# A lower half in bf16 for 38 weight parts, and another order of the work around the attention and state-space outputs

## The chip, the cores and the metric

The program runs on one core of one Trainium2 chip. Its time is that of one execution on the device, in microseconds (us). Smaller is better. Five engines work beside each other, each through its own instructions in order, and wait for each other at semaphores: TensorE (PE in the profile, with its weight loads as PEld), VectorE (DVE), ScalarE (ACT), GpSimd (POOL) and SyncE (SP), which here only starts transfers.

## The reference

256 tokens of width 1024 go through two blocks. All is float32.

```
first block:   n1 = rmsnorm(x); proj = n1 @ w_in               # q k v r, low rank, su sv, ga gb
               h = x + (sig(ga)*(gla(q,k,v,r) @ wa) + sig(gb)*(sgu(su,sv) @ wb)) @ w_out
               n2 = rmsnorm(h)
               q  = n2 @ w_q                                   # peer: 8 heads, product keys
               idx, gates = top-16 of top-16 x top-16 scores, softmax
               h += sum_k gelu(n2 . U[idx_k]) * gates_k * V[idx_k]   # 16384 experts, run densely
second block:  h += norm(swiglu(norm(h)))                      # D_FF = 2816
               q,k,v,z,xbc,dt = norm(h) @ w_in_2
               attention: 8 heads, two softmaxes each, a = p1 - lam*p2; o = norm(a @ v) per head
               state space: conv, silu, chunks of 128 tokens, 16 heads; y = norm(y*silu(z)) per group
               h += norm([o, y] @ w_out_2)
               h += norm(swiglu(norm(h)))
```

## The kernel before, in words

**Products in three passes.** Weights arrive as float32 in items of 1 MB, each of two parts of 128 x 1024 (`load`, `stream`). ScalarE rounds each part to fp32r (`round_part`, L545: `whi`), another engine subtracts that from the original and keeps the rest (`rest_part`, L562: `wlo`). Activations are split in the same way by `stream_hi` (L1335) and `stream_lo` (L1836) into `XTh` and `XTl`. `products` (L713) then makes each product of three matmuls: high weight by high activation, high by low, low by high. There are three buffers for parts (`NBUF`), so ScalarE can round part p only when TensorE has finished part p-3; and raw items sit in a ring of three, released when both lower halves are made.

**Who makes the lower halves.** VectorE does, except for the 38 parts from `S_WQ + 2` to `S_EXP + POOLED - 1` (`pooled`): 14 parts of the query matrix `peer_wq` and the first 24 expert parts, which GpSimd makes while VectorE is at the top-16 searches (L1993 to L2005). Each of these parts is a `u_part`: 8 chunks of 128 rows by three matmuls, the weight loaded as the stationary operand, 256 tokens moving. After its searches VectorE waits for the last pooled part (`part_lo`) and goes on with the selection (L2039) and with its own parts.

**Order.** Each engine's program is written out by hand. `split_to(p)` makes an engine catch up with its half of the splits up to part p at that point of its program; `take(name)` and `after(name)` first do `split_to` two parts beyond the part that the named product follows (`USE_PART`), and then wait for the product, or for its being read. Products live in PSUM banks; `MAIN` lists them in order, `MAIN_BANK` deals banks 0 to 3 out in turn, and `claim` makes TensorE wait until the one before in that bank has been read. Transposes have banks of their own (`T_BANK`, `t_claim`).

**The stage of attention and state space.** Parts of this stage are named by panel: AK (keys, four parts, `by_feature`), AV (values, four), ZZ (gate z, eight, `by_token`), WM (output matrix, twelve). TensorE runs: AK parts; decays (L1141); the scores at0 to at15 with one AV part after each four; ZZ+0 to ZZ+3 (zz0, zz1); the products inside a chunk yd0, yd1 (L1176); the state st0, st1 (L1185); three groups of transposed probabilities (L699, stage `pt`); yo0, yo1 (L1194); three more; ZZ+4; the attention products ao0, ao1 (L1203); ZZ+5 to ZZ+7; the transposed attention output; yd2, yd3; WM+0 to WM+3; the transposed state-space output (stage `ssm`); WM+4 to WM+11. `pt` uses four banks, and ScalarE copies all six groups out (L1657). `ssm` uses four banks too. VectorE makes the probabilities ready in four rounds (`normalise`, L2455 to L2467), between these its parts and bank reads (`within_tokens`, L2475, yo at L2489), then scales the attention output (L2505). ScalarE has the exponentials (L1639), the gate's silu (`z_gate`, L1649), and the squares for both norms (L1672, L1666).

Of the kernel before, what the change touches and what calls it, by code (L numbers as in the profile page):

```python
# [7 lines left out]
P = 128  # L8
# [169 lines left out]
_use(("yd0", "dve"), ("yd1", "dve"), ("st0", "act"), ("st1", "act"), ("yo0", "dve"), ("yo1", "dve"))  # L178
_part()
_use(("ao0", "dve"), ("ao1", "dve"))  # L180
_part(), _part(), _part(main="zz3"), _use(("zz2", "act"), ("zz3", "act"))
_use(("yd2", "dve"), ("yd3", "dve"))
# [10 lines left out]
SAME_BANK = {"ao0": "yo0", "ao1": "yo1"}  # L193
MAIN_BANK, _n = [], 0
for _name, _ in MAIN:
    if _name in SAME_BANK:
        MAIN_BANK.append(MAIN_BANK[MAIN_AT[SAME_BANK[_name]]])
    else:
        MAIN_BANK.append(OWN_BANK.get(_name, _n % 4))
        _n += _name not in OWN_BANK  # L200
# [19 lines left out]
def before_in(ring, n):  # L220
# [6 lines left out]
          "ffa": S_FFA - 2, "mix": S_MIX - 2, "dtt": S_MIX + 1, "xs": S_AK - 1, "bm": S_AK - 1, "pt": S_ZZ + 4, "att": S_WM - 1,  # L227
# [8 lines left out]
FOUR_BANKS = {"n1", "ya", "yb", "mg", "n2", "ffa", "mix", "pt", "ffb"}  # L236
SSM_BANKS = (6, 7, MAIN_BANK[MAIN_AT["yd2"]], MAIN_BANK[MAIN_AT["yd3"]])
T_BANK = []
for _name, _k in TSTAGES:
    for _j in range(_k):  # L240
        _i = T_AT[_name] + _j
        if _name in FOUR_BANKS:
            T_BANK.append((6, 7, 4, 5)[(_j + 2 * (_name == "yb")) % 4])
        else:
            T_BANK.append(SSM_BANKS[_j] if _name == "ssm" else 6 + _i % 2)

# [9 lines left out]


def reader_of(stage, j):

    return 1 if stage == "pt" else (T_AT[stage] + j) % 2  # L260
# [7 lines left out]
def program(nc, x, panels1, experts, ffa, panels2, ffb, cols, conv_cols, w_low, w_gate_up, w_sgu, k12, w_dt,  # L268
# [9 lines left out]
    with ctx:  # L278
# [77 lines left out]
        cut = Cut(TAIL_AT + NK * T // 2 + NBUF * PART // 2)  # L356
# [70 lines left out]
        xt_hi, xt_lo = sem("xt_hi"), sem("xt_lo")  # L427
# [65 lines left out]
        def t_read_wait(eng, i):  # L493

            for stage, pairs in TSTAGES:
                j = i - T_AT[stage]
                if 0 <= j < pairs:
                    if stage in STREAMS:
                        eng.wait_ge(xt_lo, STREAM_AT[stage] + j + 1)
                    else:  # L500
                        before = sum(1 for s2, n2 in TSTAGES if s2 not in STREAMS for k in range(n2)
                                     if T_AT[s2] + k <= i and reader_of(s2, k) == reader_of(stage, j))
                        eng.wait_ge(t_read[reader_of(stage, j)], before)
# [7 lines left out]
        def t_mine(who, stage, pairs):  # L511

            return [j for j in range(pairs) if reader_of(stage, j) == who]
# [171 lines left out]
        def _(pe):  # L685
            def transposes(stage, srcs, norm=None, waits=None, pieces=None, scales=None, pairs=None):

                for j in pairs or range((len(srcs) + 3) // 4):
# [231 lines left out]
            for h in range(PEER_H + 1):  # L920
                if h < PEER_H:
# [265 lines left out]
            read_out(pe, "av1")  # L1187
            probabilities = [PR[:, h // 2, 2 * (h % 2), P * j:P * j + P] for h in range(AT_H) for j in range(3)]
            normalised = lambda j: (att_a, (4 * j + 3) // 6 + 1)
            transposes("pt", probabilities, waits=normalised, pairs=range(3))  # L1190
# [5 lines left out]
            transposes("pt", probabilities, waits=normalised, pairs=range(3, 6))  # L1196
            token_part(["zz2", "zz3"], S_ZZ + 4, 0)
            t_read_all(pe, "pt", 6)
            for tt in range(NT):
# [23 lines left out]
        def _(act):  # L1223
# [409 lines left out]
            for r in range(4):  # L1633
                split_to(S_AV + r + 2 + max(r - 1, 0))
# [24 lines left out]
            warm_root(3)  # L1659
# [40 lines left out]
        def _(dve):  # L1700
# [286 lines left out]
            stream_lo("n2")  # L1987

# [446 lines left out]
            for r in range(4):  # L2435
# [7 lines left out]
                if r == 3:  # L2443
                    split_to(S_AV + 5)
# [4 lines left out]
                split_to(S_AV + r + 2 + 2 * (r == 3))  # L2449
# [21 lines left out]
            def within_tokens(i):  # L2471

                b = arrived(dve, f"yd{i}")
# [4 lines left out]
            normalise(1)  # L2478
            link(dve.tensor_tensor(SMALL[:, 0, :], DT[:, 0, :], ECUM[:, 2, :], ALU.mult))
            dve.tensor_tensor(by_head(XDS), by_head(XS[:, 0, :]), over_head(SMALL[:, 0, :]), ALU.mult).then_inc(xds_ready, 1)  # L2480
            normalise(2)
            within_tokens(0)
            within_tokens(1)
            normalise(3)
            split_to(S_ZZ + 4)
            for g in range(2):
                b = arrived(dve, f"yo{g}")
# [3 lines left out]
            split_to(S_ZZ + 5)  # L2491
            weights(1)
            split_to(S_ZZ + 6)

            for tt in range(NT):
                if tt:
                    split_to(S_ZZ + 7)
# [14 lines left out]
            after("zz3")  # L2512
            dve.tensor_tensor(XS[:, 0, :], XS[:, 0, :], Z[:, 0, :], ALU.mult).then_inc(ssm_gated, 1)
            split_to(S_WM + 2)
# [3 lines left out]
            link(dve.tensor_tensor(XS[:, 1, :], XS[:, 1, :], YOFF, ALU.add))  # L2518
# [99 lines left out]
```

## Time and profile before

| | |
|---|---|
| time, median of 3 runs | 1593.77 us (1591.63 to 1594.12) |
| the profiled execution's own time | 1591.63 us |
| its span, first to last instruction | 1589.9 us |
| mean granted clock of TensorE | 0.998 |
| PE busy | 1555.1 us, 98% of the span, 9128 matmuls |
| DVE busy | 1254.3 us, 79% |
| ACT busy | 806.0 us, 51% |
| POOL busy | 105.1 us, 7% |
| transfers | 270.43 MB, mean 170 GB/s |

The profile is one execution. Matmuls overlap in the pipeline, so the rate of TensorE is read from the distance of starts, not from the length of one matmul.

### The profile page before, as it was taken

To read this page: it belongs to the slowest core of one execution; us is meant where nothing else is said; L and a number is where in the kernel's file an instruction comes from. 1 tells how busy PE (TensorE), PEld (TensorE's weight loads), DVE (VectorE), ACT (ScalarE), POOL (GpSimd) and SP (SyncE) were. 2 spreads that over 40 slices of the span, in tenths; PEclk is the share of its full clock that TensorE was granted. 3 is DMA by queue.
4 is the path that set the end of the run, shared out by engine and by line. 5 is a ranking of instruction groups with operands and counts; after the bars stand their busy time and mean duration, and the time that the engine had idled before them with its cause. 6 is when DMAs were issued, how large, how long until landed. Compare 5 with 4: busy or idle time off the path is not lost.

```text
span 1589.9 us, 26306 instructions
## 1 busy us (share of the span) xinstructions
PE 1555.1 (98%) x9128; PEld 1364.0 (86%) x9128; DVE 1254.3 (79%) x2169; ACT 806.0 (51%) x1231; POOL 105.1 (7%) x67
## 2 busy tenths in 40 slices
PE   8999899999999999999999999999999999999998
PEld 7888799999999888888888888888887988778886
DVE  5575669989999777777777777888888988688877
ACT  5545545457776343344444444544445667554443
POOL 0000177700000000000000000000000000000000
PEclk9999999999999999999999999999999999999999
DMA  5545444532334555545555555555554433445552
GB/s 225 192 154 173 156 144 169 182 142 108 106 109 181 194 202 185 189 181 188 192 195 190 185 185 185 197 204 185 185 185 154 165 119 110 155 173 185 185 189 101
DMA packets 39387, 270.43 MB, mean 170 GB/s; under 512 B 4882, under 2 KB 5394, under 8 KB 7075
## 3 DMA queue, kind: packets, MB, share of 16 engines
q1 hardware_dynamic: 37440, 266.45, 47.1%
q10 hardware_dynamic: 1890, 3.24, 0.6%
q8 instruction: 34, 0.56, 0.1%
q14 instruction: 23, 0.18, 0.0%
HBM read 268.62 MB, written 1.05 MB: 170 GB/s over the span
## 4 chain that ended last, share of the span: by engine, by line
PE 79%; DVE 15%; issue 3%; ACT 2%; DVEq 1%; DMA 0%; SPq 0%; ACTq 0%
PE ps L713 51%; PE ps L746 16%; PE ps L748 7%; DVE wlo L562 2%; DVE raw L2079 2%; DVE wlo L2108 2%; PE ps L745 1%; DVE whi L2079 1%; DVE wlo L2079 1%; DVE XT L1836 1%; ACT whi L545 1%; DVE raw L2092 1%; DVE arena L2441 0%; PE ps L699 0%; PE ps L1141 0%
## 5 line engine op out<-in xcount | busy, mean ns | idle before, releaser
L746 PE MATMUL ps<-XT,whi 128*128 128x512 f32 x1200 | 429.2, 398 | 2.3 <-DVE XT L1836 1.7
L713 PE MATMUL ps<-XT,whi 128*128 128x256 f32 x1696 | 310.9, 285 | 1.1 <-DVE wlo L562 1.1
L748 PE MATMUL ps<-XT,wlo 128*128 128x256 f32 x1050 | 294.5, 280 | 0.0
L713 PE MATMUL ps<-whi,HAh 128*128 128x512 f32 x696 | 272.3, 391 | 2.4 <-DVE HAl L2267 1.4
L713 PE MATMUL ps<-wlo,HAh 128*128 128x512 f32 x696 | 271.2, 390 | 0.0
L713 PE MATMUL ps<-whi,HAl 128*128 128x512 f32 x696 | 270.8, 389 | 0.0
L545 ACT ACTIVATE whi<-raw 128x1024 fp32r<-128x1024 f32 x182 | 191.4, 1058 | 155.2 <-PE ps L713 125.8
L713 PEld LDWEIGHTS ps<-XT,whi 128*128 128x128 f32 x1696 | 263.7, 192 | 1.7 <-DVE wlo L562 1.5
L746 PEld LDWEIGHTS ps<-XT,whi 128*128 128x128 f32 x1200 | 222.5, 188 | 48.4 <-issue 2.1
L562 DVE TENSOR_TENSOR wlo<-raw,whi 128x1024 fp32r<-128x1024 f32 x162 | 196.6, 1222 | 72.4 <-ACT whi L545 70.7
L713 PE MATMUL ps<-XT,wlo 128*128 128x256 f32 x848 | 239.8, 283 | 0.0
L1559 ACT ACTIVATE whi<-raw 128x1024 fp32r<-128x1024 f32 x108 | 114.7, 1062 | 175.2 <-PE ps L746 114.3
L748 PEld LDWEIGHTS ps<-XT,wlo 128*128 128x128 f32 x1050 | 198.2, 189 | 5.7
L713 PE MATMUL ps<-whi,XT 128*128 128x512 f32 x592 | 184.7, 393 | 3.3 <-DVE XT L1836 1.4
L2306 DVE TENSOR_TENSOR wlo<-raw,whi 128x1024 fp32r<-128x1024 f32 x108 | 132.0, 1222 | 49.6 <-ACT whi L1559 48.3
L713 PEld LDWEIGHTS ps<-XT,wlo 128*128 128x128 f32 x848 | 162.4, 191 | 0.0
L713 PEld LDWEIGHTS ps<-wlo,HAh 128*128 128x128 f32 x696 | 130.6, 188 | 28.1
L713 PEld LDWEIGHTS ps<-whi,HAl 128*128 128x128 f32 x696 | 130.7, 188 | 27.9
L713 PEld LDWEIGHTS ps<-whi,HAh 128*128 128x128 f32 x696 | 130.9, 188 | 27.4 <-issue 3.3
L713 PEld LDWEIGHTS ps<-whi,XT 128*128 128x128 f32 x592 | 109.5, 188 | 30.3 <-issue 4.7
L2176 DVE TENSOR_TENSOR wlo<-raw,whi 128x1024 fp32r<-128x1024 f32 x108 | 130.8, 1221 | 1.1
L713 PE MATMUL ps<-wlo,XT 128*128 128x512 f32 x296 | 115.4, 390 | 0.0
(293 smaller groups left out, 1919.5 us busy)
## 6 DMA issues: line engine op xcount, KB each, us to landing
raw<-in_experts SPq DMA_DIRECT2D x128, 1024.0 KB, 4.8
raw<-in_panels SPq DMA_DIRECT2D x58, 1024.0 KB, 4.8
raw<-in_ffa SPq DMA_DIRECT2D x33, 1024.0 KB, 4.7
raw<-in_ffb SPq DMA_DIRECT2D x33, 1024.0 KB, 4.8
arena<-in_row_post ACTq DMA_DIRECT2D x3, 512.0 KB, 4.7
X<-in_x SPq DMA_DIRECT2D x2, 512.0 KB, 5.2
arena<-in_row_ln ACTq DMA_DIRECT2D x2, 256.0 KB, 4.2
arena<-in_row_post SPq DMA_DIRECT2D x1, 512.0 KB, 5.6
```

The lines of the kernel that those rows point to most:

```text
L545: act.activation(whi[:, buf(p), :], half(item_of(p), p % 2), ACT.Copy).then_inc(part_hi, 1)
L562: eng.tensor_tensor(low_weights(p), half(item_of(p), p % 2), whi[:, buf(p), :].bitcast(f32), ALU.subtract).then_inc(part_lo, 1)
L713: last = pe.matmul(out, x if w_moving else w, w if w_moving else x, start=start and n == 0, stop=stop and n == 2)
L745: pe.matmul(out[:, T:], wl[:, k], XTh[:, k], start=False, stop=False)
L746: last = pe.matmul(out, wh[:, k], XT[:, k], start=k == 0, stop=k == NK - 1)
L748: pe.matmul(out[:, T:], wl[:, k], XTh[:, k], start=False, stop=False)
L1559: act.activation(whi[:, buf(q), :], half(item_of(q), q % 2), ACT.Copy)\
L1836: last = dve.scalar_tensor_tensor(lo, t_bank(stage, j)[:, T * q:T * q + T], col(gain, k) if gain else 1.0, hi.bitcast(f32), ALU.mult, ALU. ...
L2079: return dve.tensor_tensor(out, iota.bitcast(f32).unsqueeze(1).broadcast_to(shape), idx[:, bass.ds(g * ONES, n)].unsqueeze(2).broadcast_to ...
L2108: dve.tensor_tensor(wlo[:, buf(p), :], half(item_of(p), p % 2), whi[:, buf(p), :].bitcast(f32), ALU.subtract).then_inc(part_lo, 1)
L2176: dve.tensor_tensor(wlo[:, buf(p + j), :], half(item_of(p), j), whi[:, buf(p + j), :].bitcast(f32), ALU.subtract).then_inc(part_lo, 1)
L2306: dve.tensor_tensor(wlo[:, buf(q), :], half(item_of(q), q % 2), whi[:, buf(q), :].bitcast(f32), ALU.subtract).then_inc(part_lo, 1)
```

## The change

It has two parts. First, the 38 pooled parts get a lower half in bf16 (`WB1`) in place of fp32r, VectorE makes a bf16 copy of the high activations (`XB1`, 128 x 2048) once, and the third pass multiplies these two. TensorE waits for that copy at the second query panel. Second, the order of the attention and state-space stage differs: which part is split where, which product comes when, which bank it has, and who copies the transposed probabilities out. The diff is condensed: calls stand side by side, and some bodies are named instead of printed.

```diff
 # banks and bookkeeping
-_use(("yd0","dve"), ("yd1","dve"), ("st0","act"), ("st1","act"), ("yo0","dve"), ("yo1","dve"))
-_part()
-_use(("ao0","dve"), ("ao1","dve"))
-_part(), _part(), _part(main="zz3"), _use(("zz2","act"), ("zz3","act"))
-_use(("yd2","dve"), ("yd3","dve"))
+_use(("yd0","dve"), ("yd1","dve"), ("st0","act"), ("st1","act"))
+_by_token("zz2", "zz3", "act")
+_use(("yo0","dve"), ("yo1","dve"), ("ao0","dve"), ("ao1","dve"), ("yd2","dve"), ("yd3","dve"))
-SAME_BANK = {"ao0": "yo0", "ao1": "yo1"}
-# pt: four banks, read by ScalarE alone; ssm: banks 6, 7 and those of yd2, yd3
+# pt and ssm: banks 6 and 7 in turn; pt read by VectorE and ScalarE in turn
 # bf16
+        XB1 = cut(NK * T // 2).bitcast(bf16).rearrange("p (k t) -> p k t", k=NK)
+        WB1 = cut(NBUF * PART // 2).bitcast(bf16).rearrange("p (b n) -> p b n", b=NBUF)
 def low_weights(p):
+            if pooled(p):
+                return WB1[:, buf(p), :]
             return wlo[:, buf(p), :]
 def third_acts(p):
+            if pooled(p):
+                return XB1
             return XTh
 # TensorE
+                if h == 1:
+                    pe.wait_ge(xt_b, 1)
 ...
-            read_out(pe, "av1");  transposes("pt", probabilities, pairs=range(3))
+            by_token(["zz2", "zz3"], S_ZZ + 4)
             read_out(pe, "st1");  yo0, yo1
-            transposes("pt", probabilities, pairs=range(3, 6))
-            token_part(["zz2", "zz3"], S_ZZ + 4, 0)
+            transposes("pt", all six)
             t_read_all(pe, "pt", 6);  ao0, ao1
-            for j in range(1, 4):
-                token_part(["zz2", "zz3"], S_ZZ + 4, j)
+            within_tokens(1)
             pe.wait_ge(att_y, 1)
             transposes("att", tiles(AOUT, 4))
-            within_tokens(1)
 # ScalarE
-                split_to(S_AV + r + 2 + max(r - 1, 0))
+                split_to(S_AV + r + 2 + (r == 3))
 ...            z_gate(0); st0, st1
+            z_gate(1)
+            warm_root(3)
             pt copies (now every second one)
-            warm_root(3)
             for tt in range(NT):  ao square
-                split_to(S_ZZ + 7)
             head_root(2, 16)
-            act.activation(warm[4], ident[:, 0:1], ACT.Silu)
-            z_gate(1)
+            ssm_squares(0)
             stream_hi("att")
-            warm_root(0)
-            ssm_squares(0)
 # VectorE
             stream_lo("n2")
+            dve.tensor_copy(XB1, XTh.bitcast(f32)).then_inc(xt_b, 1)
 ...            XSKIP, c = 0, 1
-                if c == 0:
-                    split_to(S_AK + 2)
 ...            scores
-                if r == 3:
-                    split_to(S_AV + 5)
-                split_to(S_AV + r + 2 + 2 * (r == 3))
+                split_to(S_AV + r + 2)
             normalise(0)
-            normalise(1);  xds
-            normalise(2);  within_tokens(0), (1)
-            normalise(3);  split_to(S_ZZ + 4);  yo reads;  split_to(S_ZZ + 5)
-            weights(1);  split_to(S_ZZ + 6)
+            split_to(S_ZZ + 2);  xds;  split_to(S_ZZ + 3)
+            normalise(1);  split_to(S_ZZ + 4)
+            normalise(2);  split_to(S_ZZ + 5);  within_tokens(0), (1)
+            normalise(3);  split_to(S_ZZ + 6)
+            weights(1);  split_to(S_ZZ + 7)
+            after("zz3");  XS0 * Z0;  yo reads
+            pt copies 0, 2, 4
             attention sums, head_scale, AOUT, stream_lo("att")
-            after("zz3");  XS0 * Z0;  split_to(S_WM + 2)
             within_tokens(2), (3);  + YOFF
-            XS1 * Z1;  split_to(S_WM + 3)
+            split_to(S_WM + 3);  XS1 * Z1
```

## Rows read from the trace of the kernel before

**Rows 1.** Windows: length; busy PE, PEld, DVE, ACT, POOL; granted clock; transfer share; GB/s.

```profile
237.00:337.00 100.00, 100.00 (x837) 100.00 (x836) 94.95 (x331) 48.02 (x70) 63.26 (x26) 1.00 0.51 179
1292.00:1372.00 80.00, 78.36 (x471) 63.67 (x470) 66.16 (x120) 56.39 (x131) 0.00 (x0) 1.00 0.29 107
```

**Rows 2.** Timeline of PE, query panels and experts: start, us, operation [idle before].

```profile
222.89 0.28 PE L713 MATMUL ps<-XT,wlo 128*128 128x256 f32 x1
...
228.28 0.28 PE L713 MATMUL ps<-XT,wlo 128*128 128x256 f32 x1
...
599.38 0.39 PE L713 MATMUL ps<-wlo,HAh 128*128 128x512 f32 x1
...
605.50 0.39 PE L713 MATMUL ps<-wlo,HAh 128*128 128x512 f32 x1
```

**Rows 3.** Timelines of DVE and POOL, first block.

```profile
210.19 0.88 DVE L1993 MAX8 arena<-arena 128x8 f32<-128x128 f32 x4 [11.23 <-ACT arena L1412]
...
257.55 2.40 POOL L562 TENSOR_TENSOR wlo<-raw,whi 128x1024 fp32r<-128x1024 f32 x1 [0.26 <-ACT whi L545]
...
314.87 1.43 DVE L2039 SCALAR_TENSOR_TENSOR arena<-arena 128x256 bf16<-128x256 f32 x4 [2.63 <-POOL wlo L562]
...
348.82 0.42 DVE L2058 COPY sel<-ps 128x256 f32<-128x256 f32 x1 [1.33 <-PE ps L699]
```

**Rows 4.** Timelines of PE and DVE at the AK parts.

```profile
1280.20 0.48 PE L713 MATMUL ps<-XT,whi 128*128 128x256 f32 x2
...
1284.69 1.22 DVE L562 TENSOR_TENSOR wlo<-raw,whi 128x1024 fp32r<-128x1024 f32 x1
1285.82 1.22 DVE L2427 TENSOR_TENSOR arena<-arena 128x1024 f32<-128x1024 f32 x1
```

**Rows 5.** Timeline of DVE from the last scores to the attention output.

```profile
1315.73 2.36 DVE L562 TENSOR_TENSOR wlo<-raw,whi 128x1024 fp32r<-128x1024 f32 x2
1317.99 0.20 DVE L2455 RECIPROCAL arena<-arena 128x8 f32<-128x8 f32 x1
...
1320.86 0.20 DVE L2455 RECIPROCAL arena<-arena 128x8 f32<-128x8 f32 x1
...
1327.94 1.28 DVE L2475 TENSOR_TENSOR arena<-arena,ps 128x512 f32<-128x512 f32 x2
...
1344.02 1.29 DVE L2505 TENSOR_TENSOR arena<-ps,arena 128x512 f32<-128x512 f32 x2
```

**Rows 6.** Timeline of ACT, third round of exponentials and the splits after it.

```profile
1310.59 0.39 ACT L1639 ACTIVATE arena<-arena 128x128 f32<-128x128 f32 x1
...
1314.10 2.16 ACT L545 ACTIVATE whi<-raw 128x1024 fp32r<-128x1024 f32 x2
```

**Rows 7.** Timeline of PE through the stage.

```profile
1323.10 3.68 PE L1176 MATMUL ps<-arena 128*128 128x64 f32 x32
...
1328.38 1.47 PE L699 MATMUL ps<-ident,arena 128*128 128x128 f32 x12
1329.69 1.88 PE L1194 MATMUL ps<-arena 128*128 128x512 f32 x4
...
1336.22 5.46 PE L1203 MATMUL ps<-arena 128*128 128x64 f32 x48
...
1349.79 1.03 PE L699 MATMUL ps<-ident,arena 128*128 128x128 f32 x8
...
1354.15 0.71 PE L713 MATMUL ps<-whi,XT 128*128 128x512 f32 x2
...
1365.66 1.91 PE L699 MATMUL ps<-ident,arena 128*128 128x128 f32 x16
1368.26 0.70 PE L713 MATMUL ps<-whi,XT 128*128 128x512 f32 x2 [0.70 <-DVE XT L1836]
```

**Rows 8.** Windows after two gaps of PE, the columns of rows 1.

```profile
1220.00:1222.00 2.00, 2.00 (x11) 1.88 (x10) 2.00 (x6) 1.71 (x5) 0.00 (x0) 0.50 0.00 0
...
1394.00:1396.00 2.00, 1.36 (x11) 0.92 (x10) 1.68 (x4) 1.57 (x4) 0.00 (x0) 1.00 0.00 0
```

More of the change, by code:

```diff
@@ L177 @@
 _by_token("zz0", "zz1", "act")
-_use(("yd0", "dve"), ("yd1", "dve"), ("st0", "act"), ("st1", "act"), ("yo0", "dve"), ("yo1", "dve"))
-_part()
-_use(("ao0", "dve"), ("ao1", "dve"))
-_part(), _part(), _part(main="zz3"), _use(("zz2", "act"), ("zz3", "act"))
-_use(("yd2", "dve"), ("yd3", "dve"))
+_use(("yd0", "dve"), ("yd1", "dve"), ("st0", "act"), ("st1", "act"))
+_by_token("zz2", "zz3", "act")
+_use(("yo0", "dve"), ("yo1", "dve"), ("ao0", "dve"), ("ao1", "dve"), ("yd2", "dve"), ("yd3", "dve"))
 assert _parts == S_WM
@@ L192 @@
 OWN_BANK = {"av0": 4, "av1": 5, "wm0": 4, "wm1": 5}
-SAME_BANK = {"ao0": "yo0", "ao1": "yo1"}
 MAIN_BANK, _n = [], 0
 for _name, _ in MAIN:
[L196 to L200, printed above, removed]
+    MAIN_BANK.append(OWN_BANK.get(_name, _n % 4))
+    _n += _name not in OWN_BANK
 I_G, I_PRE = EXP0 + FIRST // 2, EXP0 + EARLY // 2
@@ L234 @@
     _n += _k
-FOUR_BANKS = {"n1", "ya", "yb", "mg", "n2", "ffa", "mix", "pt", "ffb"}
-SSM_BANKS = (6, 7, MAIN_BANK[MAIN_AT["yd2"]], MAIN_BANK[MAIN_AT["yd3"]])
+FOUR_BANKS = {"n1", "ya", "yb", "mg", "n2", "ffa", "mix", "ffb"}
 T_BANK = []
@@ L241 @@
         _i = T_AT[_name] + _j
[L242 to L245, printed above, removed]
+        T_BANK.append((6, 7, 4, 5)[(_j + 2 * (_name == "yb")) % 4] if _name in FOUR_BANKS else 6 + _i % 2)
 STREAMS = {"n1": (0, "norm1"), "ya": (0, "gla"), "yb": (4, None), "mg": (0, None), "n2": (0, "norm2"),
@@ L511, in t_mine @@
         def t_mine(who, stage, pairs):
-            return [j for j in range(pairs) if reader_of(stage, j) == who]
+            return [j for j in range(pairs) if (T_AT[stage] + j) % 2 == who]
         def item_of(p):
@@ L685, in _, with transposes @@
         def _(pe):
-            def transposes(stage, srcs, norm=None, waits=None, pieces=None, scales=None, pairs=None):
-                for j in pairs or range((len(srcs) + 3) // 4):
+            def transposes(stage, srcs, norm=None, waits=None, pieces=None, scales=None):
+                for j in range((len(srcs) + 3) // 4):
                     t_claim(pe, stage, j)
@@ L1186, in _ @@
                           stop=True).then_inc(main_done, 1)
[L1187 to L1190, printed above, removed]
+            by_token(["zz2", "zz3"], S_ZZ + 4)
             read_out(pe, "st1")
@@ L1195, in _ @@
                           stop=True).then_inc(main_done, 1)
-            transposes("pt", probabilities, waits=normalised, pairs=range(3, 6))
-            token_part(["zz2", "zz3"], S_ZZ + 4, 0)
+            transposes("pt", [PR[:, h // 2, 2 * (h % 2), P * j:P * j + P] for h in range(AT_H) for j in range(3)],
+                       waits=lambda j: (att_a, (4 * j + 3) // 6 + 1))
             t_read_all(pe, "pt", 6)
+            read_out(pe, "av1")
             for tt in range(NT):
@@ L2471, in within_tokens @@
             def within_tokens(i):
[L2473 removed]
+                b = take(f"yd{i}")
                 c, half_c = i // 2, slice(512 * (i % 2), 512 * (i % 2) + 512)
@@ L2484, in _ @@
             normalise(3)
-            split_to(S_ZZ + 4)
+            split_to(S_ZZ + 6)
+            weights(1)
+            split_to(S_ZZ + 7)
+            after("zz3")
+            dve.tensor_tensor(XS[:, 0, :], XS[:, 0, :], Z[:, 0, :], ALU.mult).then_inc(ssm_gated, 1)
             for g in range(2):
-                b = arrived(dve, f"yo{g}")
+                b = take(f"yo{g}")
                 e = ECUM[:, 1, 8 * g:8 * g + 8].unsqueeze(2).broadcast_to([P, 8, SSM_P])
```

31 lines of the change are left out of this document (14 added, 17 removed).

## The prediction, made before the changed kernel ran

> **What bounds the kernel now.** I read the page's busy times first, then windows, then the timelines of single engines. TensorE is the bound almost everywhere, and in both places that the change touches: between 237 and 337 us, in the pooled parts, it is busy for all of the 100 us, and between 1292 and 1372 us for 78.36 of 80 [rows 1]. So two things count: what shortens TensorE's own work, and what makes it wait. The second window also says how little a better order could give there: 1.6 us of idle time.
>
> **Part one, the bf16 pass.** A part in the pooled stretch is 24 matmuls of 256 columns. Third-pass matmuls start at 222.89 and 15 triplets later at 228.28, 5.39 / 45 = 0.120 us each. With 512 columns, 27 matmuls take 605.50 - 599.38 = 6.12 us, 0.227 each [rows 2]. The difference is 0.107 us per 256 columns, so each matmul costs its columns plus a fixed 0.0133 us. The columns stay, and bf16 can take away at most the fixed piece. The changed matmuls are 38 parts x 8 chunks = 304, so the gain lies between 0 and 304 x 0.0133 = 4.0 us. No row shows a bf16 matmul, or says how much of the fixed piece belongs to the four-byte operands. It stands at both widths, so it is not streaming, and the operand's size is what changes: I take three quarters, 0.010 us and **-3.0 us** in all, and keep 0 and 4.0.
>
> The Trainium skill has a price for this (TensorE: Matmul & The Clock Gate, section on the 56 ns): a warm bf16 matmul starts N / 2.4 GHz + about 2.5 ns after the one before. By it the step is 0.109 us and the gain 304 x 0.0108 = 3.3 us. The same page (Weight-path perf modes) has bf16 weights of 128 columns loaded faster than float32 ones, which cannot take the step below its columns; no run here shows either yet.
>
> Is the gain kept? GpSimd needs 2.40 us a part and the shortest gap before one is 0.26 [rows 3], 2.66 us, against a new TensorE period of 24 x 0.120 - 8 x 0.010 = 2.80 us. It keeps up if writing bf16 costs it no more than 0.14 us. VectorE waits 2.63 us for the last pooled part at 314.87, so it can follow up to that much, and at 348.82 it sits waiting for TensorE's transposes after its selection, so it is not what is late there [rows 3]. The new copy of 128 x 2048 is bounded by twice a 128 x 1024 subtraction, 2 x 1.22 = 2.4 us; it lies in VectorE's 11.23 us of idle time before 210.19 [rows 3], which begins at 198.96 with the last streamed activation. TensorE takes these chunks up as they come, so at least one of the first panel's two parts (2.88 us) lies behind that moment and covers the copy. Cost nothing; without that cover, 2.4 us once, in front of the searches and in front of TensorE. TensorE's wait for it has nothing late behind it.
>
> **Part two, the order.** Here I walk the new programs through with the durations of the rows, in the time of the trace before. Units: a VectorE split 1.13 us (1315.73 to 1317.99 for two), one round of `normalise` 2.87 (1317.99 to 1320.86), reading two banks 1.2, one bank 0.6 [rows 5]; a round of exponentials 3.5 (1310.59 to 1314.10), a rounding by ScalarE 1.08 [rows 6]; a `by_token` part 12 x 0.227 = 2.72, yd plus st 5.28 (1323.10 to 1328.38), yo 1.7, ao 5.3, att transposes and yd 4.36 (1349.79 to 1354.15) of which yd is 3.5, the ssm stage 2.6 until WM+4 starts [rows 7].
>
> *AK+2.* TensorE starts this part at 1280.20 + 2 x 2.88 = 1285.96, and its lower half is made 1284.69 to 1285.91, just in time [rows 4]. The change puts the XSKIP product, 1.13 us, in front. TensorE starts at 1287.1: **+1.1**. The scores follow TensorE, so all behind it moves along.
>
> I leave this 1.1 out of the times that follow.
>
> *ZZ+0 to ZZ+3.* They start at 1323.10 - 4 x 2.72 = 1312.2 and every 2.72 us. ZZ+1 is wanted at 1314.9. ScalarE now rounds it behind the third exponentials, and these can start only one rounding sooner: I take them 1310.0 to 1313.5, ZZ+1 rounded at 1314.6. VectorE splits it until 1315.8: TensorE waits 0.9 and ends it at 1318.6. `normalise(0)` comes in between, and ZZ+2 is split at 1318.6 to 1319.8: wait 1.3. xds takes until 1321.1; ScalarE has the fourth exponentials, the AV copies, then ZZ+3 rounded at about 1321.3; VectorE splits by 1322.5; TensorE wants it at 1322.6. ZZ+3 ends at 1325.3 instead of 1323.10: **+2.2**.
>
> *zz2's bank.* yd and st run to 1330.6. zz2 and zz3 now lie in the banks of yd0 and yd1. VectorE, from 1322.4 with two rounds (5.74), two splits (2.26) and the reads (1.2), frees them at 1331.6: wait **+1.1**. Then ZZ+4 to ZZ+7 run 1331.7 to 1342.6, split in time.
>
> *The transposed probabilities.* VectorE must wait for zz3's silu (1343.5, a pipeline's end and 0.6 behind the last part), multiply (1.13), read yo (1.2) and only then copy pair 0, by 1346.5. TensorE has finished yo and two pairs at 1345.2 and the next pair needs that bank: wait 1.3. With two banks each further pair needs the copy before it, then the last must be copied before the attention products: 0.5 and 0.9 more. Sum **+2.7**; ao starts at 1349.65. Before, four banks and ScalarE alone hid it behind yo.
>
> *Attention output.* ao ends at 1354.95, yd2 and yd3 at 1358.45. The scaled output came 3.8 us after ao (1341.5 to 1345.3 [rows 5, 7]), so 1358.75: wait 0.3. Before, yd2 and yd3 lay between the att transposes and WM+0 and hid the streaming; now TensorE waits for it. The ssm stage shows that distance, 2.6 us from first transpose to next part: WM+0 starts at 1361.35 instead of 1354.15. The lateness was 6.0 (2.2 + 1.1 + 2.7); it is now 7.2: **+1.2**.
>
> *ssm with two banks.* WM+0 to WM+3, 4 x 2.72, end at 1372.2; the y scales are ready just before. Pair 2 then waits for the low half of pair 0, pair 3 for that of pair 1, 3.7 us in place of 2.6, and WM+4 starts at 1375.9 instead of 1368.26, 7.6 late: **+0.4**, since the stretch before WM+4 already held 0.6 us of waits (1354.15 to 1365.66 is 11.5 for 10.9 of work) that the late start swallows. WM+5 is split behind the stream, **+0.2**.
>
> Sum of the order: 1.1 + 2.2 + 1.1 + 2.7 + 1.2 + 0.4 + 0.2 = **+8.9 us**. A walk may be off by a wait or two of about 1.3 each: 6.5 to 11.
>
> **Total.** -3.0 + 8.9 = +5.9. The profiled execution took 1591.63 us for a span of 1589.9, so 1597.5 on its own time. The median of the runs is 2.1 above it: 1593.77 + 5.9 = **1599.7 us**, 0.37% slower.
>
> **The rivals.**
> (a) *The clock falls.* After the feed-forward before this stage, TensorE had a gap with only transposes in it, and the granted clock was 0.50 at 1220 to 1222, the 1.2 GHz level; after a similar gap at 1392 it stayed at 1.00 [rows 8]. In my walk the pt, att and ssm stretches each have 2 to 3 us of waits with nothing but transposes between. Half clock over some 4 us costs 2 us: 1601.7. For it: the same shape of gap; against: the even record. The Trainium skill (TensorE: Matmul & The Clock Gate, Part 4) says that a transpose does not count as TensorE being busy; by that rule the fall is likelier than the record says, and the time would be this one.
> (b) *bf16 changes nothing on TensorE.* The fixed piece stays at 0.0133: 1593.8 + 8.9 = 1602.7. For it: weights and moving columns are still 128 and 256, and two passes of three keep fp32r. Against: nothing else can explain why the piece is the same at both widths.
> (c) *GpSimd becomes the pace.* It decides from 2.54 us a part on. At a fifth more, 2.88 + 0.26 = 3.14 us against 2.88 now, 36 parts cost +9 instead of -3: 1612. Against: it writes half the bytes.
> (d) *The other side: not slower.* VectorE, idle for long stretches after 1338, is not late: it reaches yd0 before TensorE ends st (before 1330.6; my walk has 1331.6) and pair 0 before TensorE ends pair 1 (before 1345.2; my walk has 1346.5). Then the waits for zz2's bank and for pair 0, and those that follow from it, fall away, 1.1 + 2.7. The order costs 5.1, the whole +2.1: 1595.9, which a measurement cannot tell from no change; with the bf16 gain at its bound of 4.0 it is +1.2, and it is faster only if the stream waits go too. VectorE's chain is fixed in order, and at either place a whole us would have to be found, so this is unlikely.
>
> **How the numbers follow.** A difference of 0.2%, 3.2 us, is about what a measurement of this kernel can tell from no change. Forecast 0.50; (a) 0.20; (b) 0.10; (c) 0.05; (d) 0.12, all of it within 0.2%; faster, by (d) with everything going well, 0.03. Of the forecast a twentieth is left for an order that costs 6 or less. So slower 0.83, same 0.14, faster 0.03. The range takes in (a), (b) and most of (d), and the order's bounds: 1595.5 to 1605.
>
> **What would show it.** In the changed profile the third pass has bf16 operands and steps of 0.110 instead of 0.120 beside 0.120 for the others, a pooled part takes 2.80 us, and VectorE's wait before L2039 is near nothing. PE waits for DVE's splits at AK+2, ZZ+1 and ZZ+2 (0.9 to 1.3 each), for the reads of yd, for copies of L699's pairs, and before WM+0 for XT. The window from AK to WM+4 is 9 us longer. The prediction is wrong if the 0.0133 stays or GpSimd's part exceeds 2.54 us, or if VectorE and ScalarE are ahead of TensorE at the banks of yd0 and pair 0.

## The result, and the profile after

The changed kernel takes 1605.99 us in the median of five runs (1603.14 to 1611.96), the kernel before 1592.99 us (1591.63 to 1594.12) in its five beside it. The ratio is 1.0068, with a 95% interval of 1.0054 to 1.0084: slower, by 10.8 us. It is smaller than the 13.0 us between the two medians because it takes in all 31 executions of the changed kernel (1601.08 to 1611.96, median 1603.59), and not only these five. The forecast was +5.9 us. On the 1593.77 us that it was made against, the ratio gives 1604.6, inside the range of 1595.5 to 1605 by 0.4 us; the median of the five stands 1 us above it. The profiled execution took 1603.59 us for a span of 1601.8, with a mean granted clock of 0.994 where before had 0.998.

First the bf16 pass. PE's timeline of the changed kernel in the query panels, which answers to [rows 2]:

```profile
221.41 0.28 PE L703 MATMUL ps<-arena 128*128 128x256 bf16 x1
221.45 0.48 PE L703 MATMUL ps<-XT,whi 128*128 128x256 f32 x2
221.77 0.28 PE L703 MATMUL ps<-arena 128*128 128x256 bf16 x1
...
222.85 0.28 PE L703 MATMUL ps<-arena 128*128 128x256 bf16 x1
```

Four triplets lie between 221.41 and 222.85, so one takes 0.36 us and a matmul still 0.120 on average. Nothing has become shorter. The weight load of that pass has, in the groups of weight loads (line, operation, shapes, count | busy us, mean ns | idle before):

```profile
L703 PEld LDWEIGHTS ps<-XT,whi 128*128 128x128 f32 x1696 | 263.8, 193 | 2.9 <-DVE wlo L552 1.5 <-issue 1.3
...
L703 PEld LDWEIGHTS ps<-arena 128*128 128x128 bf16 x304 | 28.9, 95 | 12.8
```

It takes 95 ns instead of 193, but loads lie beside the matmuls, and the step does not follow them. The windows of the changed kernel (columns of [rows 1]) have TensorE busy for all of the pooled stretch, as before:

```profile
237.00:337.00 100.00, 100.00 (x838) 90.53 (x837) 94.88 (x342) 48.73 (x71) 64.22 (x27) 1.00 0.50 175
...
190.00:200.00 10.00, 7.47 (x46) 6.92 (x45) 5.74 (x15) 5.79 (x15) 0.00 (x0) 0.83 0.30 106
```

The second of these rows is code that both kernels share, and its granted clock is 0.83: it fell to 0.50 there for 3.4 us, and once more near 167 us. The profile of the kernel before has neither fall. The timelines of DVE and POOL, which answer to [rows 3]:

```profile
201.13 1.22 DVE L1973 CAST arena<-XT 128x2048 bf16<-128x2048 f32 x1
212.47 0.87 DVE L1979 MAX8 arena<-arena 128x8 f32<-128x128 f32 x4 [10.11 <-ACT arena L1400]
...
259.89 2.40 POOL L552 TENSOR_TENSOR arena<-raw,whi 128x1024 bf16<-128x1024 f32 x1 [0.30 <-ACT whi L531]
...
317.21 1.43 DVE L2025 SCALAR_TENSOR_TENSOR arena<-arena 128x256 bf16<-128x256 f32 x4 [2.64 <-POOL arena L552]
```

The copy of the activations took 1.22 us and is hidden: 10.11 us of idle time are left behind it. GpSimd writes bf16 in the same 2.40 us. VectorE waits 2.64 us for the last pooled part, as it did before (2.63), since no part has become shorter.

Then the order. PE's timeline from the AK panel to WM+5, which answers to [rows 4, 7]; brackets hold the idle time before an instruction and its releaser:

```profile
1282.57 0.48 PE L703 MATMUL ps<-XT,whi 128*128 128x256 f32 x2
...
1289.68 0.47 PE L703 MATMUL ps<-XT,whi 128*128 128x256 f32 x2 [1.13 <-DVE wlo L552]
...
1319.61 0.73 PE L703 MATMUL ps<-whi,XT 128*128 128x512 f32 x2 [0.88 <-DVE wlo L552]
1323.62 0.72 PE L703 MATMUL ps<-whi,XT 128*128 128x512 f32 x2 [0.99 <-DVE wlo L552]
1329.21 3.68 PE L1168 MATMUL ps<-arena 128*128 128x64 f32 x32
...
1335.34 0.70 PE L703 MATMUL ps<-whi,XT 128*128 128x512 f32 x2 [0.68 <-DVE arena L2457]
1346.34 1.88 PE L1183 MATMUL ps<-arena 128*128 128x512 f32 x4
...
1350.34 1.09 PE L689 MATMUL ps<-ident,arena 128*128 128x128 f32 x8 [1.25 <-DVE arena L2483]
1351.78 1.09 PE L689 MATMUL ps<-ident,arena 128*128 128x128 f32 x8 [0.35 <-DVE arena L2483]
1353.56 5.57 PE L1193 MATMUL ps<-arena 128*128 128x64 f32 x48 [0.69 <-ACT arena L1647]
...
1362.87 1.09 PE L689 MATMUL ps<-ident,arena 128*128 128x128 f32 x8 [0.17 <-DVEq L2499]
1365.48 0.70 PE L703 MATMUL ps<-whi,XT 128*128 128x512 f32 x2 [1.52 <-issue]
1379.00 1.44 PE L689 MATMUL ps<-ident,arena 128*128 128x128 f32 x8 [1.47 <-DVE XT L1821]
1383.57 0.74 PE L703 MATMUL ps<-whi,XT 128*128 128x512 f32 x2 [0.36 <-DVE wlo L552]
```

The reader should see two things. Every wait of the prediction is there, at the place it named. And the AK panel itself starts 2.37 us later than before (1282.57 against 1280.20), ahead of all changed order. So the measure for the order is the distance from the start of the AK panel to the start of WM+5: 101.00 us here, and 91.45 before, where WM+5 started so:

```profile
1371.65 0.74 PE L713 MATMUL ps<-whi,XT 128*128 128x512 f32 x2 [0.39 <-DVE wlo L562]
```

The order costs 9.55 us in this execution; the sum had 8.9. Below, that distance is called **AK to WM+5**. Behind WM+5 nothing differs: 1601.8 - 1383.57 = 218.2 us are left to the end of the span, and 1589.9 - 1371.65 = 218.3 before. So the spans of the two profiled executions differ by 11.9 us: 9.55 by the order, and 2.4 ahead of the AK panel, where the two falls lie. splits_back below, which has neither of these falls, starts its panel at 1280.70.

### The profile page after: what moved, and what is told of

The parts are those of the page before. It is cut to its first block, busy times and chain, and to the rows that moved or that the text cites. A ratio compares the mean times of both kernels' runs of the same rounds, so it can differ in the third digit from the quotient of the medians.

```text
span 1601.8 us, 26306 instructions
## 1 busy us (share of the span) xinstructions
PE 1560.6 (97%) x9128; PEld 1354.8 (85%) x9128; DVE 1257.6 (79%) x2173; ACT 802.7 (50%) x1224; POOL 105.4 (7%) x67
## 4 chain that ended last, share of the span: by engine, by line
PE 80%; DVE 14%; issue 3%; ACT 2%; DVEq 1%; DMA 0%; ACTq 0%
PE ps L703 52%; PE ps L736 16%; PE ps L738 7%; DVE wlo L552 2%; DVE wlo L2094 2%; DVE raw L2065 2%; PE ps L735 1%; DVE wlo L2065 1%; DVE whi L2065 1%; PE ps L689 1%; DVE XT L1821 1%; ACT whi L531 0%; DVE arena L2425 0%; PE ps L955 0%; PE ps L1133 0%
## 5 line engine op out<-in xcount | busy, mean ns | idle before, releaser
L738 PE MATMUL ps<-XT,wlo 128*128 128x256 f32 x1050 | 294.5, 280 | 0.0
L531 ACT ACTIVATE whi<-raw 128x1024 fp32r<-128x1024 f32 x182 | 191.4, 1057 | 163.0 <-PE ps L703 133.8
L738 PEld LDWEIGHTS ps<-XT,wlo 128*128 128x128 f32 x1050 | 198.3, 189 | 5.7
L1547 ACT ACTIVATE whi<-raw 128x1024 fp32r<-128x1024 f32 x108 | 114.7, 1062 | 175.2 <-PE ps L736 114.3
L703 PE MATMUL ps<-XT,wlo 128*128 128x256 f32 x544 | 153.8, 283 | 0.0
L1479 ACT ACTIVATE whi<-raw 128x1024 fp32r<-128x1024 f32 x60 | 63.8, 1063 | 99.4 <-PE ps L703 99.4
```

Source lines behind the costliest of these rows:

```text
L531: act.activation(whi[:, buf(p), :], half(item_of(p), p % 2), ACT.Copy).then_inc(part_hi, 1)
L703: last = pe.matmul(out, x if w_moving else w, w if w_moving else x, start=start and n == 0, stop=stop and n == 2)
L738: pe.matmul(out[:, T:], wl[:, k], XTh[:, k], start=False, stop=False)
L1479: act.activation(whi[:, buf(p), :], half(item_of(p), p % 2), ACT.Copy).then_inc(part_hi, 1)
L1547: act.activation(whi[:, buf(q), :], half(item_of(q), q % 2), ACT.Copy)\
```

## Experiments

**The bf16 pass alone, and the order alone.** The first is the kernel before with the hunks of `XB1` and `WB1` and nothing else, the second is the changed kernel without them:

```diff
 bf16_only: the kernel before
+            if pooled(p): return WB1[:, buf(p), :]      # low_weights
+            if pooled(p): return XB1                    # third_acts
+            dve.tensor_copy(XB1, XTh.bitcast(f32)).then_inc(xt_b, 1)
 order_only: the changed kernel
-            the same lines
```

> The kernel before with the bf16 third pass of the pooled parts alone. My theory after the result: three bf16 matmuls among fp32r ones keep the step of 0.120 us (a triplet stays at 0.36 us, a pooled part at 2.88), so the time is that of before, within 0.1% (1592 to 1594 us where before has 1593). The rival, the forecast of the prediction: the gain is real but hidden in the changed kernel by something else, a triplet takes 0.350 us, a part 2.80 and the time is 3.0 us shorter, ratio 0.998.

> The changed kernel with its third pass put back to fp32r, so the new order alone. My theory: all of the loss is the order, WM+5 starts 9.5 us later after the start of the AK panel than it did before, and the time is that of the whole change, ratio 1.006 (1601 to 1604 us, where a fall of the granted clock outside the changed code adds or takes about 2 us). The rival, that the bf16 pass gives 3.0 us which the order of the changed kernel loses too: ratio 1.008 to 1.009.

The bf16 pass alone: 1593.22 us against 1593.87, ratio 0.9999 (0.999 to 1.0008); AK to WM+5 is 91.41. It neither gives nor costs, as expected. The order alone: 1604.69 us, ratio 1.0073 (1.0061 to 1.0086), that of the whole change. Its profile has an AK to WM+5 of 102.53 us, and there the windows of PE (length, busy, granted clock, transfers) show why it is 1.5 more than in the changed kernel:

```profile
1364.00:1366.00 2.00, 1.34 (x11) 1.00 0.00 0
...
1368.00:1370.00 2.00, 2.00 (x6) 0.50 0.00 0
```

The granted clock fell to 0.50, the 1.2 GHz level, at WM+0, behind the attention products and the transposes. So the clock does fall in this stage in this execution, as in the prediction's rival (a).

**Where the fixed piece of a matmul sits.** The bf16 matmuls kept the 0.120 us step of the fp32r ones. Two kernels ask what holds it there. The first is the changed kernel, new order included, with every pass of the pooled parts in bf16; it leaves out the products with the high halves of those parts, so its output is another one. The second keeps the computation, and puts the eight bf16 matmuls of a part behind its sixteen fp32r ones.

```diff
 bf16_probe: the changed kernel, u_part
+                if pooled(p): wh = wl
+                acts = (x3[:, k],) * 3 if pooled(p) else (XTh[:, k], XTl[:, k], x3[:, k])
 bf16_grouped: the kernel before with the bf16 pass, u_part
+                if pooled(p):
+                    for k in range(NK):
+                        chunk_in(k)
+                        pe.matmul(out, wh[:, k], XTh[:, k], start=k == 0, stop=False)
+                        pe.matmul(out, wh[:, k], XTl[:, k], start=False, stop=False)
+                    for k in range(NK):
+                        last = pe.matmul(out, wl[:, k], x3[:, k], start=False, stop=k == NK - 1)
+                    return last
```

> The changed kernel in which all three passes of the pooled parts take bf16 weights and bf16 activations, so that every matmul of these parts is bf16; it leaves out the products with the high-rounded weights and the activations' streamed halves, whose places bf16 products of the same size take. If the fixed piece of 0.0133 us belongs to the operands' size and a neighbour in fp32r keeps it alive, the step falls to 0.107 to 0.110 and a part from 2.88 to 2.57 to 2.64 us. If the fixed piece belongs to every matmul whatever its type, the step stays 0.120 and the part 2.88. Where GpSimd needs 2.40 + 0.26 us a part, a faster TensorE shows as its waits for GpSimd's or VectorE's, of at most 0.1 us a part.

> The kernel before with the bf16 third pass, and in each pooled part the eight bf16 matmuls in a row behind the sixteen fp32r ones. The runs so far have a bf16 matmul at 0.120 us between fp32r ones and at 0.109 where all are bf16. Theory: what counts is the matmul next to it, so seven of the eight take 0.109, a part 2.80 us instead of 2.88, and 38 parts save 2.9 us: ratio 0.998, 1590 to 1591 us where before has 1593 to 1594. Rival one: fp32r work anywhere in the part keeps 0.120, or the change of type costs it again at the two borders, no gain, ratio 1.000. Rival two: GpSimd, at 2.66 us a part, or VectorE cannot follow, and TensorE's idle time grows by what the step gives.

PE's timeline of the first kernel:

```profile
254.81 4.42 PE L703 MATMUL ps<-arena 128*128 128x256 bf16 x39
```

39 matmuls take 4.42 us, of which the last has 0.28: (4.42 - 0.28) / 38 = 0.109 us each. The fixed piece falls from 0.0133 to about 0.002 when the neighbours are bf16 as well. The time was 1591.92 us in its one execution, 11.7 us below the changed kernel's profiled one; 38 parts of 24 such matmuls, 0.011 us less each, make 10 of these. The Trainium skill (TensorE: Matmul & The Clock Gate, section on the 56 ns) gives N / 2.4 GHz plus about 2.5 ns, an estimate of 0.109 us for 256 columns: the trace agrees, for bf16 beside bf16.

And PE's timeline of the second:

```profile
253.80 1.05 PE L743 MATMUL ps<-arena 128*128 128x256 bf16 x8
254.60 0.36 PE L740 MATMUL ps<-XT,whi 128*128 128x256 f32 x1
254.80 0.28 PE L741 MATMUL ps<-XT,whi 128*128 128x256 f32 x1
...
256.59 1.05 PE L743 MATMUL ps<-arena 128*128 128x256 bf16 x8
257.39 0.36 PE L740 MATMUL ps<-XT,whi 128*128 128x256 f32 x1
```

One part, from 254.60 to 257.39, takes 2.79 us instead of 2.88. That is 16 x 0.120 + 8 x 0.109, so the two changes of type in a part cost nothing. This kernel takes 1590.38 us against 1592.17, ratio 0.9983 (0.9974 to 0.9992), about 2.7 us, where 38 parts at 0.09 each make 3.4: the theory, that the matmul next to it counts, was right, and this kernel is faster than both. What it is in an fp32r neighbour that holds the step up, no run shows. AK to WM+5 is 91.37, so the gain lies ahead of the stage. The last wait of VectorE for a pooled part fell from 2.63 to 2.42 only, and GpSimd kept up.

**One wait made alone.** The kernel before, with the second XSKIP product ahead of the split of AK+2:

```diff
 ak_only: the kernel before
                 ins = dve.tensor_tensor(by_head(XSKIP[:, c, :]), ...)
-                if c == 0:
-                    split_to(S_AK + 2)
```

> The kernel before with one product by XSKIP moved in front of the split of AK+2. Both theories of the walk have TensorE wait for that split once: about 1.1 us (the changed kernel showed 1.13) at AK+2, and all that follows 1.1 us later up to WM+5. The rival: before WM+5 there is slack that takes it back, and WM+5 stands as far from the start of AK as in the kernel before.

```profile
1283.26 0.49 PE L713 MATMUL ps<-XT,whi 128*128 128x256 f32 x2
...
1290.38 0.48 PE L713 MATMUL ps<-XT,whi 128*128 128x256 f32 x2 [1.12 <-DVE wlo L562]
...
1375.94 0.72 PE L713 MATMUL ps<-whi,XT 128*128 128x512 f32 x2 [0.38 <-DVE wlo L562]
```

AK to WM+5 is 1375.94 - 1283.26 = 92.68, 1.23 more than before. Nothing behind it takes the wait back: the theory was right, its rival not. The panel starts late here too (1283.26), with clock falls in the same shared code; distances are free of that.

**Three moves undone one at a time, from the changed kernel.**

```diff
 splits_back: roundings and splits of ZZ and AV in the places they had before
-                split_to(S_AV + r + 2 + (r == 3))              # ScalarE
+                split_to(S_AV + r + 2 + max(r - 1, 0))
-                split_to(S_AV + r + 2)                         # VectorE
+                split_to(S_AV + r + 2 + 2 * (r == 3))          # and S_AV + 5 ahead of the last read
 pt_four: four banks for the transposed probabilities, ScalarE copies all six groups
 ssm_four: four banks for the ssm transposes
```

> The changed kernel with ScalarE's roundings and VectorE's splits of the ZZ and AV parts in the places that they had before. Theory: the waits of 0.88 and 0.99 us at ZZ+1 and ZZ+2 vanish, and VectorE then stands later at the bank of zz2 (0.68 us before): WM+5 is 1.5 to 2 us earlier. Rival: VectorE's chain is what is late behind it, the waits move on to the bank of zz2 and to pair 0, and less than 0.5 us comes back.

> The changed kernel with four banks for the transposed probabilities, all copied by ScalarE, as before. Theory: the waits of 1.25, 0.35 and 0.69 us of the changed trace come from VectorE, which reaches pair 0 late; without them the attention products start about 2.3 us earlier, but what follows (the scaled output, the streaming, the y scales) is late by itself and takes some of it back: WM+5 stands 1.3 us earlier behind the start of the AK panel than in the changed kernel (99.7 instead of 101.0 us). Rival one: all 2.3 come back. Rival two: ScalarE with four copies is as late as VectorE was, and nothing comes back.

> The changed kernel with four banks for the ssm transposes. Theory: the wait of 1.47 us before WM+4 goes and with it 1.1 us of the time up to WM+5. Rival: the y scales or the streaming of the lower halves are what is late there, and the wait moves to the next chunk with less than 0.3 us gained.

| kernel | AK starts | WM+5 starts | AK to WM+5 | against the change |
|---|---|---|---|---|
| before | 1280.20 | 1371.65 | 91.45 | -9.55 |
| the change | 1282.57 | 1383.57 | 101.00 | |
| splits_back | 1280.70 | 1381.51 | 100.81 | -0.19 |
| pt_four | 1283.57 | 1382.76 | 99.19 | -1.81 |
| ssm_four | 1283.28 | 1383.15 | 99.87 | -1.13 |

ssm_four gave what was expected (1.1). pt_four gave 1.81, between the 1.3 of its theory and the 2.3 of its first rival. splits_back gave almost nothing, against a theory of 1.5 to 2. PE's timeline of splits_back at zz2:

```profile
1333.32 0.69 PE L703 MATMUL ps<-whi,XT 128*128 128x512 f32 x2 [3.00 <-DVE arena L2459]
```

The waits of 0.88 and 0.99 at ZZ+1 and ZZ+2 are gone, and the wait for the bank of zz2 has grown from 0.68 to 3.00. Its releaser is the read of yd0 by VectorE. DVE's timeline of the changed kernel has that read here:

```profile
1333.95 1.28 DVE L2457 TENSOR_TENSOR arena<-arena,ps 128x512 f32<-128x512 f32 x2
```

It starts 51.38 us behind AK. In splits_back it starts at 1331.95, 51.25 behind AK. So VectorE's chain up to that read keeps its length, and TensorE waits for its end in one place or in three. In the kernel before the read started 1327.94 - 1280.20 = 47.74 us behind AK [rows 4, 5]. The 3.5 to 3.6 us between are the wait at AK+2 (1.2) and two splits of 1.13: by the diffs, VectorE has made the lower halves up to ZZ+3 ahead of this read in the kernel before, and up to ZZ+5 in the changed one and in splits_back. PE's timeline of pt_four, and that of ssm_four:

```profile
1352.78 5.57 PE L1198 MATMUL ps<-arena 128*128 128x64 f32 x48 [0.95 <-ACT arena L1652]
```

```profile
1379.76 0.70 PE L707 MATMUL ps<-whi,XT 128*128 128x512 f32 x2 [0.70 <-DVE XT L1825]
```

In pt_four the three waits of 1.25, 0.35 and 0.69 have become one of 0.95. In ssm_four the wait before WM+4 is 0.70, exactly that of the kernel before [rows 7].

**Is it the bank?** This is splits_back with zz2 and zz3 in the banks of av0 and av1:

```diff
 zz_own: splits_back, and
-OWN_BANK = {"av0": 4, "av1": 5, "wm0": 4, "wm1": 5}
+OWN_BANK = {"av0": 4, "av1": 5, "zz2": 4, "zz3": 5, "wm0": 4, "wm1": 5}
```

> The changed kernel with the ZZ and AV splits where they were before, and with zz2 and zz3 in the banks of av0 and av1 instead of those of yd0 and yd1. With the splits alone TensorE waited 3.00 us at zz2's bank for VectorE's read of yd0, and WM+5 came only 0.2 us earlier. Theory: that wait is the bank's; without it zz2 starts 3.0 us earlier, the sixth split (ZZ+6) then comes about 1.4 us late, and 1.5 us or more are gained up to WM+5 (99.3 us or less behind the start of AK, against 100.8). Rival: VectorE's whole chain is late, all 3.0 us move on to the splits and to pair 0, and WM+5 gains under 0.3 us.

```profile
1340.40 0.73 PE L703 MATMUL ps<-whi,XT 128*128 128x512 f32 x2 [1.46 <-DVE wlo L552]
1343.81 0.73 PE L703 MATMUL ps<-whi,XT 128*128 128x512 f32 x2 [0.39 <-DVE wlo L552]
...
1353.88 5.57 PE L1193 MATMUL ps<-arena 128*128 128x64 f32 x48 [0.69 <-ACT arena L1647]
```

The wait of 3.00 is gone, and 1.46 and 0.39 stand at ZZ+6 and ZZ+7. The attention products start 1353.88 - 1283.82 = 70.06 us behind AK, where splits_back has 70.84: 0.8 gained, between theory and rival. The other 2.2 are VectorE's chain again. Behind that point the granted clock fell at WM+0, as in the order alone, and AK to WM+5 is 101.66; that part cannot be compared.

**Four moves undone together.** Splits, both sets of banks, and the split of AK+2. What stays is the sequence: zz2 and zz3, then yo, all the transposed probabilities, the attention products and yd2, yd3 in a row. Before, three ZZ parts lay between the attention products and yd2.

> The changed kernel with four of its moves undone together: the split of AK+2 between the XSKIP products, the ZZ and AV roundings and splits, four banks for the transposed probabilities, four for the ssm transposes. What stays is zz2 and zz3 in front of yo, the probabilities' transposes behind them, and the attention products behind those. Theory, by the single runs: -1.1 (the AK wait) -0.2 -1.8 -1.15, so WM+5 stands 96.7 us behind the start of the AK panel instead of 101.0 (91.45 before), and 5.3 us of the loss belong to the new sequence itself, with a wait of about 3 us at zz2's bank. Rival: each undone wait comes back at the next place where VectorE is late, and more than 98.5 us stay.

> The same kernel as all_back. In its one execution the granted clock was 0.50 for 19 us in the attention stretch, so that WM+5 stood 106.7 us behind the start of AK, while the waits before that were those expected. Theory: that was an accident of this execution; over the rounds the granted clock is 0.994 to 0.997 as in the changed kernel, WM+5 stands 96.7 us behind AK in a profile without such a fall, and the median is 5 to 6 us above that of before, ratio 1.003 to 1.004. Rival: the new sequence, with long runs of narrow products of 64 columns between waits, brings such a fall most of the time: mean clock 0.991 or less, ratio 1.006 or more, and the undone moves gain nothing in the median.

The kernel took 1609.62 us in its single execution and 1607.49 us (1607.22 to 1610.52, four runs) against 1593.90: ratio 1.0094 (1.0077 to 1.011). That is not faster than the change's 1.0068; the two intervals overlap, so that it is slower is not shown. AK to WM+5 is 106.68 and 106.64. PE's timeline of the second:

```profile
1332.26 1.19 PE L712 MATMUL ps<-whi,XT 128*128 128x512 f32 x2 [3.02 <-DVE arena L2470]
...
1350.24 8.37 PE L1202 MATMUL ps<-arena 128*128 128x64 f32 x48 [0.95 <-ACT arena L1656]
1358.40 7.03 PE L1177 MATMUL ps<-arena 128*128 128x64 f32 x32
...
1368.24 1.19 PE L712 MATMUL ps<-whi,XT 128*128 128x512 f32 x2 [1.10 <-issue]
```

and its windows, with all engines (columns of [rows 1]):

```profile
1332.00:1335.00 3.00, 2.74 (x7) 2.19 (x8) 2.90 (x12) 0.00 (x0) 0.00 (x0) 0.52 0.88 336
...
1354.00:1372.00 18.00, 16.90 (x71) 15.75 (x71) 7.25 (x14) 4.67 (x11) 0.00 (x0) 0.50 0.00 0
```

The waits are the expected ones. But the 48 attention products take 8.37 us instead of 5.57 and yd2, yd3 7.03 instead of 3.74, at a granted clock of 0.50 that lasts from 1353 to 1373. The price, by distances: from zz2 to yo 12.53 us where the change has 11.00, from the attention products to WM+0 18.00 where pt_four has 11.92, from WM+0 to WM+5 19.29 where ssm_four has 16.97. That is 1.5 + 6.1 + 2.3 = 9.9 us, and 106.64 - 9.9 = 96.7 is what the waits alone had promised. The theory was right on the waits and wrong on the time. The rival's numbers hold for this kernel: all five executions have a mean clock of 0.989 or less, where the kernel before had 0.993 to 0.998. Its reason is not shown. pt_four has the same row of work, 24 transposes, a wait of 0.95, the 48 attention products, yd2 and yd3, and the windows of its profile (columns as for the order alone) stay at full clock through it:

```profile
1350.00:1360.00 10.00, 9.05 (x82) 1.00 0.14 56
1360.00:1370.00 10.00, 8.31 (x49) 1.00 0.00 0
```

So that row alone does not bring the fall. Nor does a wait of 3.0 us at zz2 alone: splits_back has one, with its clock at 1.00. Both profiles with the four moves undone have the two together, first a fall of 3.4 us at zz2 and then the long one. Which of the differences to pt_four brings it, the wait at zz2, the split of AK+2 or the ssm banks, or whether pt_four's one execution was lucky, stays open. The Trainium skill (TensorE: Matmul & The Clock Gate, Part 4) says that a transpose does not count as TensorE being busy in the way that a product does. The long fall begins inside products of 64 columns that follow 24 transposes, but pt_four has the same without a fall, and no run here takes the transposes and the narrow products apart.

**Filling the gaps.** The kernel before with 26 matmuls of 512 columns in gaps of TensorE; their products are used nowhere.

```diff
 before_fill: the kernel before
+            def fill(out, n):
+                for k in range(n):
+                    pe.matmul(out, XTh[:, k % NK, 0:P], XT[:, k % NK], start=True, stop=True)
+            fill(bank("wq0"), 10)             # ahead of the n2 transposes
+            fill(t_bank("mix", 0), 9)         # ahead of those of mix
+            fill(t_bank("ffb", 0), 7)         # ahead of those of ffb
```

> The kernel before with 26 further matmuls of 512 columns into banks that the next transposes overwrite: 10 ahead of the n2 transposes, 9 ahead of the mix transposes, 7 ahead of those of ffb, all in TensorE's gaps. Their products are used nowhere. Theory: the granted clock falls to 0.50 (at 194, 1220 and 1392 us of the spans so far, in one run and not in the next) because TensorE stands idle or has only transposes just before; with the fillers those three falls are gone, each is worth about 1.7 us where it occurs, and the median is 2 to 4 us shorter, ratio 0.998, with the clock at 0.997 or more. The fall at 167 us may stay. Rival: the falls are not tied to what TensorE does just there, they stay or move, and the time is the same or longer by what the fillers delay the transposes, up to 1 us each.

PE's timeline and a window of it, at the gap of [rows 8]:

```profile
1214.57 2.20 PE L829 MATMUL ps<-XT 128*128 128x512 f32 x9
```

```profile
1220.00:1222.00 2.00, 1.58 (x14) 1.00 0.00 0
```

The granted clock there is 1.00 instead of 0.50, and up to the end of the work no window of 10 us of this profile is below 1.00 before 1580; all eleven executions have a mean clock of 0.998 or 0.999. The time is 1592.38 against 1593.72 us, ratio 0.9993 (0.9984 to 1.0002): not to be told from no change. The theory had the falls right and their price wrong, which it put at 2 to 4 us in all. So the falls are tied to what TensorE does, and those in gaps are cheap: from the wait at 1211 to the ffb transposes the kernel before, with its one fall, took 1392.88 - 1211.49 = 181.39 us, and this one 1392.53 - 1211.73 = 180.80. That fall cost 0.6 us. PE's timelines of the kernel before and of this one show why, at the first product behind the transposes:

```profile
1220.84 0.77 PE L713 MATMUL ps<-XT,HAh 128*128 128x256 f32 x2
```

```profile
1221.08 0.47 PE L713 MATMUL ps<-XT,HAh 128*128 128x256 f32 x2 [0.42 <-DVE XT L1846]
```

Both stand 9.35 us behind that wait. At half clock the transposes filled 0.4 us in which TensorE otherwise waits for VectorE; only the few products up to the end of the fall cost time.

## Why the prediction came out as it did

- **The sign and the cause of the loss: right.** The new order alone gives the whole loss (ratio 1.0073), by waits for VectorE. That the number fell into the range owes something to luck: +10.8 us is nearly twice the +5.9 forecast, 1604.6 lies nearer to rival (b)'s 1602.7 than to the forecast's 1599.7, and the range was wide enough to take in (b).
- **Part one, -3.0 us: wrong, it is 0.** The step that failed is "It stands at both widths, so it is not streaming, and the operand's size is what changes: I take three quarters". The operand's size does count (0.109 where all are bf16), but not for a single bf16 matmul between two fp32r ones, where the step stays 0.120. Rival (b) had this, at 0.10, and so did the lower bound of the term. What spoke for it was known: two of three passes keep fp32r. What was held against it, that nothing else can explain the piece, is answered by the two kernels above: the piece goes only where the neighbours are bf16 too.
- **Its cover: right.** GpSimd at 2.40 us a part, the copy hidden under VectorE's idle time, no loss (0.9999).
- **Part two, +8.9 us: 9.55.** By starts of matmuls, less the work between them (and, up to WM+0, less the 0.9 us of waits that the kernel before had on that way), measured against predicted: AK+2 1.35 (1.1), to yd0 2.39 more (2.2), to zz2 0.85 (1.1), yo to the attention products 2.9 (2.7), to WM+0 1.4 (1.2), to WM+5 0.6 (0.6), and 0.1 between zz2 and yo. For example AK+2: 1289.68 - 1282.57 is 7.11, less two parts of 2.88. Each wait costs 0.1 to 0.3 us more than its idle time shows, because a matmul is drawn as 0.28 us long where the next one starts 0.120 behind it.
- **The reason behind the ZZ term: wrong.** The prediction gave +2.2 to the splits and +1.1 to zz2's bank as things of their own. Undoing the splits gave 0.19, since the bank's wait took 3.00. It is one debt, VectorE's chain up to the read of yd0 with two more splits in it, collected in three places.
- **The transposed probabilities and the ssm banks: right**, 1.81 and 1.13 when undone; the first includes less than the term of 2.7, since 0.95 is then waited for ScalarE's six copies.
- **Rival (a), the clock: underrated in kind.** The profile of the change shows no fall in this stage, and the forecast, not (a), is nearer in mechanism. But of the nine profiles with the new sequence (that of the all-bf16 parts is one) four have a fall in the stage, and of the five with the old sequence none. Its price of 2 us fits the single fall (1.5 in the order alone); with the moves undone it was 9.9.
- **What no term held.** 10.8 - 9.55 = 1.3 us. Part of it can be chance in the five executions of the kernel before: their median is 1592.99, while beside the experiments it was 1592.17 to 1593.90, so the change's 1603.59 stands 9.7 to 11.4 us above it. The executions of the change range from 1601.1 to 1612.0 us, with mean clocks of 0.997 to 0.988, so falls in this stage in some of them are another likely cause. How much each holds is not shown. And the shared code falls at about 167 and 194 us in nine of fourteen profiles, in kernels of both kinds, which is why single profiles differ by 2 to 3 us ahead of any change.
- **Rivals (c) and (d):** did not come. GpSimd stayed at 2.40, VectorE was late at both places.

## What to carry to other kernels

A cheaper type in one pass of several gives nothing while it alternates with the dearer one; put its matmuls in a row, which here turned 0 into 2.7 us at no other cost. When several waits name one engine, undo one and see whether the next grows before adding them up. And look at the clock before believing a sum of waits: with four moves undone the waits fell as planned, by 4.3 us up to WM+5, and two falls of the granted clock took back twice that. Every profile with a fall in this stage has the new sequence, in which no wide part stands between transposes and narrow products, but another profile has the same row at full clock, so what brings them is open.

## What the runs showed of the hardware that was not expected

- A bf16 matmul of 256 columns costs 0.120 us between two fp32r ones (0.36 for the three) and 0.109 us in a row of bf16 ones.
- Undoing four costly moves gained nothing, 1607.49 against 1605.99 us, because of the granted clock: one fall of 3.4 us behind a wait of 3.0 us, and one of about 20 us, through work that stayed at full clock in pt_four.
- With 26 idle-time matmuls in three gaps the mean clock was 0.998 or 0.999 in every execution, where the kernel before had 0.993 to 0.998 beside it, and the time did not fall measurably (ratio 0.9993).
